# Last of eight experts written out, its rows placed by TensorE, and the meta rows dropped from layer two

## What is computed

```python
def first_block(x, meta_tokens, ...):
    h = jnp.concatenate([meta, x], axis=1)          # 16 + 256 rows
    for layer in range(2):                          # hybrid_layer
        h = hybrid_layer(h, ...)                    # q, k, v, z projections, causal attention of
                                                    # 4 "diff" and 8 "fox" heads, out projection
    return rms_norm(h, final_g)[:, N_META:]         # the 16 meta rows are dropped here

def second_block(x, ...):
    for l in range(2):
        x = x + mixers(rms_norm(x)) @ w_out[l]      # pooling, gated, convolution
        h = rms_norm(x)
        x = x + (swiglu(h) if l == 0 else moe_swiglu(h, ...))
    return rms_norm(x, final_g)

def moe_swiglu(h, router, wg, wu, wd):              # 8 experts, inner width 3584, top 2
    top_v, top_i = lax.top_k(t @ router, 2)
    top_w = softmax(top_v)
    for e in range(8):
        out = out + gates[:, e:e+1] * swiglu(t, wg[e], wu[e], wd[e])
```

## Time and profile before

| what | value |
|---|---|
| median of 3 runs | 1765.38 us (1765.19 to 1765.78) |
| the profiled execution, its own time | 1765.0 us |
| its span, first to last instruction | 1763.2 us |
| PE busy | 1686.0 us (96%), 10014 instructions |
| DVE, ACT, POOL busy | 1408.5, 1152.2, 253.0 us |
| DMA | 476.86 MB, mean 270 GB/s |
| granted TensorE clock, mean | 0.981 |

### The profile page before, as it was taken

The page is one execution under the profiler, slowest core; times in us unless marked ns, Lnnn a source line. Parts: engine busy times, 40 slices in busy tenths (PEclk is TensorE's granted clock), DMA queues, the critical chain, the costliest instruction groups (busy, mean ns, idle before and its releaser), DMA issues.

```text
span 1763.2 us, 27386 instructions
## 1 busy us (share of the span) xinstructions
PE 1686.0 (96%) x10014; PEld 1480.7 (84%) x10014; DVE 1408.5 (80%) x1607; ACT 1152.2 (65%) x1297; POOL 253.0 (14%) x261
## 2 busy tenths in 40 slices
PE   8999899989899999899999999999999999999993
PEld 7888898889799999788888888888888888888883
DVE  7666666759866667868898898988998988989885
ACT  5563555456654446677777777777777777777773
POOL 2212022128310003600010010000100100101000
PEclk9999999999899999999999999999999999999997
DMA  7322442245455464359999999999999999999993
GB/s 302 120 85 85 160 139 97 72 155 182 162 173 191 131 214 152 126 195 378 379 368 373 379 387 365 372 391 385 360 391 387 375 374 372 385 378 367 393 386 132
DMA packets 71329, 476.86 MB, mean 270 GB/s; under 512 B 8405, under 2 KB 9077, under 8 KB 19413
## 3 DMA queue, kind: packets, MB, share of 16 engines
q1 hardware_dynamic: 67781, 463.25, 70.0%
q0 software_dynamic: 3184, 11.55, 1.8%
q10 hardware_dynamic: 288, 1.05, 0.1%
HBM read 469.53 MB, written 6.29 MB: 270 GB/s over the span
## 4 chain that ended last, share of the span: by engine, by line
PE 75%; issue 9%; DVE 8%; ACT 3%; POOL 3%; DMA 1%; SPq 0%; DVEq 0%; POOLq 0%; ACTq 0%
PE bank L451 24%; PE bank L453 23%; PE bank L452 23%; DVE wlo L442 2%; ACT whi L437 2%; PE bank L1096 1%; POOL cacc L2234 1%; DVE msb L1747 1%; DVE bank L1777 1%; DVE sm L1667 0%; PE bank L730 0%; DMA ys<-y_slots 0%; POOL pr L2150 0%; PE bank L674 0%; PE bank L1068 0%
## 5 line engine op out<-in xcount | busy, mean ns | idle before, releaser
L442 DVE TENSOR_TENSOR wlo<-raw,whi 128x2048 fp32r<-128x2048 f32 (+2 forms) x453 | 1000.8, 2219 | 177.7 <-ACT whi L437 176.5
L437 ACT ACTIVATE whi<-raw 128x2048 fp32r<-128x2048 f32 (+2 forms) x453 | 838.0, 1850 | 219.0 <-PE bank L453 218.8
L451 PE MATMUL bank<-whi,hthi 128*128 128x512 f32 x896 | 354.1, 395 | 1.7 <-DVE htlo L2077 1.7
L453 PE MATMUL bank<-whi,htlo 128*128 128x512 f32 x896 | 350.1, 391 | 0.0
L452 PE MATMUL bank<-wlo,hthi 128*128 128x512 f32 x896 | 349.7, 390 | 0.0
L451 PE MATMUL bank<-uhi,whi 128*128 128x272 f32 (+2 forms) x1072 | 315.1, 294 | 4.0 <-DVE wlo L442 3.5
L453 PE MATMUL bank<-uhi,wlo 128*128 128x272 f32 (+2 forms) x1072 | 306.3, 286 | 0.0
L452 PE MATMUL bank<-ulo,whi 128*128 128x272 f32 (+2 forms) x1072 | 305.8, 285 | 0.0
L451 PEld LDWEIGHTS bank<-uhi,whi 128*128 128x128 f32 (+1 forms) x1072 | 201.9, 188 | 7.2 <-DVE wlo L442 4.8
L452 PEld LDWEIGHTS bank<-ulo,whi 128*128 128x128 f32 (+1 forms) x1072 | 202.3, 189 | 0.7
L453 PEld LDWEIGHTS bank<-uhi,wlo 128*128 128x128 f32 (+1 forms) x1072 | 202.1, 189 | 0.0
(11 more groups left out here) (354 smaller groups left out, 2128.6 us busy)
## 6 DMA issues: line engine op xcount, KB each, us to landing
raw<-in_wm SPq DMA_DIRECT2D x338, 1024.0 KB, 7.1
raw<-in_w SPq DMA_DIRECT2D x66, 1024.0 KB, 5.0
raw<-in_w SPq DMA_DIRECT2D x18, 768.0 KB, 4.3
raw<-in_w SPq DMA_DIRECT2D x16, 704.0 KB, 4.2
raw<-in_w SPq DMA_DIRECT2D x14, 512.0 KB, 3.6
ys<-y_slots SPq DMA_DIRECT2D x4, 512.0 KB, 5.3
raw<-in_w SPq DMA_DIRECT2D x2, 576.0 KB, 3.7
hT<-in_hT SPq DMA_DIRECT2D x2, 544.0 KB, 6.1
```

The costliest lines, as they stand in the source:

```text
L437: act.activation(whi[:, n % RING, 0:c], raw[:, n % RAW, 0:c], ACT.Copy).then_inc(hi_ready, 1)
L442: dve.tensor_tensor(wlo[:, n % RING, 0:c], raw[:, n % RAW, 0:c], whi[:, n % RING, 0:c].bitcast(F32), ALU.subtract).then_inc(lo_ready, 1)
L451: pe.matmul(out, s_hi, m_hi, start=start, stop=False, skip_group_check=shared)
L453: return pe.matmul(out, s_lo, m_hi, start=False, stop=stop, skip_group_check=shared)
```

## The change

1. *Layer two without meta rows.* In the second attention layer the q and z tiles, the output projection, and all that follows from them take columns 16 to 271 only (256 in place of 272), and the query tile of 16 rows is left out of scores, mask, exponent, scaling, turning and products. k, v and the logits keep 272.
2. *The last expert is written out.* All loops run seven turns; the eighth expert follows as straight code with `last=True`. It loads no ninth expert's units and gathers nothing. Ahead of it ACT and DVE read the count into a register. Its last two units are multiplied one output half at a time (`down_by_halves`), so both units must be split before the first product.
3. *Its rows reach the tokens through PE.* Its `yt` isn't scattered. PE turns its `pick` at chunk 4, DVE copies that to `pickT`, and after the last half PE makes four products (`place`) of `pickT` with `yt`, which DVE adds to `xt`.
4. *Other rows are added early.* SP loads `ys` behind its last weight unit, and DVE adds the slots to `xt` (`settle`) ahead of the last `yt`. Since the last expert's slots are not written any more, `y_slots` is cleared by POOL with four DMAs of 512 KB when the first mixer is done.
5. *The end.* Square sums are taken in halves of 512 columns, POOL scales the first half's sum, ACT loads its root table early.
6. The second loop keeps its place behind the branch and now prepares its own first expert.

```diff
+            take = leaving(l) if TILE_OF[i][0] in "qz" else slice(0, LEN)
             for k in range(KD):
-                    mm = three_pass(pe, bank[i % 2][:, 0:LEN], hi[:, k, cols], lo[:, k, cols],
-                                    uhi[:, k, :], ulo[:, k, :], k == 0, k == KD - 1)
+                    mm = three_pass(pe, bank[i % 2][:, take], hi[:, k, cols], lo[:, k, cols],
+                                    uhi[:, k, take], ulo[:, k, take], k == 0, k == KD - 1)
...
-            with sp.Fori(0, EXPERTS) as it:
+            with sp.Fori(0, LAST) as it:
                 expert(it)
-            sp.wait_ge(scattered, EXPERTS + 1)
+            expert(LAST, 0)
+            sp.wait_ge(scattered, EXPERTS)
+            load_rows()
             sp.wait_ge(count_ready, 1)
...
+                def down_by_halves(c):
+
+                    pe.wait_ge(atlo_ready, it * CHUNKS + (c + 1))
+                    views = [weights(EXPERT_UNITS.index(("down", c, part))) for part in range(2)]
+                    for half in range(2):
+                        cols = slice(half * 512, (half + 1) * 512)
+                        for part, (hi, lo) in enumerate(views):
+                            for i in range(2):
+                                f = 2 * part + i
+                                mm = three_pass(pe, bank[5 + half][:], athi[:, c % 2, f, :], atlo[:, c % 2, f, :], hi[:, i, cols], lo[:, i, cols],
+                                                False, f == 3)
+                        mm.then_inc(unit_done, 1)
...
+            def place():
+
+                pe.wait_ge(rows_ready, 5)
+                for tt in range(2):
+                    for half in range(2):
+                        pe.wait_ge(yt_ready, EXPERTS + half)
+                        pe.matmul(bank[2 * tt + half][:], pickT[:, tt * P:(tt + 1) * P], yt[:, half * 512:(half + 1) * 512],
+                                  start=True, stop=True).then_inc(placed, 1)
...
+            act.wait_ge(count_ready, 1)
+            fullest = act.value_load(cnti[0:1, 0:1], min_val=0, max_val=SEQ)
+            expert(LAST, True)
+            act.activation(warm[:, 7:8], eps[:], ACT.Sqrt)
             with act.If(fullest > P):
...
+            def settle(tt, times=1):
+
+                step = 4 * (times - 1) + 2 * tt
+                dve.wait_ge(ys_landed, 16 * 2 * TOP_K * times)
+                dve.tensor_tensor(ys[:, tt, 0, :], ys[:, tt, 0, :], ys[:, tt, 1, :], ALU.add).then_inc(result_step, 1)
+                dve.wait_ge(result_step, step + 1)
+                dve.tensor_tensor(xt[:, tt, :], xt[:, tt, :], ys[:, tt, 0, :], ALU.add).then_inc(result_step, 1)
...
             fullest = dve.value_load(cnti[0:1, 0:1], min_val=0, max_val=SEQ)
+            expert(LAST, True)
+            for tt in range(2):
+                dve.wait_ge(result_step, 2 * tt + 2)
+                for half in range(2):
+                    dve.wait_ge(placed, 2 * tt + half + 1)
+                    own = xt[:, tt, half * 512:(half + 1) * 512]
+                    dve.tensor_tensor(own, own, bank[2 * tt + half][:], ALU.add).then_inc(sum_ready, 1)
+            dve.wait_ge(sum_ready, 4)
             with dve.If(fullest > P):
...
+                if L == 0:
+                    pool.wait_ge(unit_done, UNIT_FF)
+                    pool.memset(zero[:], 0.0).then_inc(const2_ready, 1)
+                    pool.wait_ge(const2_ready, CONST2 + 1)
+                    clear_slots(zero)
```

## The result

The changed kernel takes 1740.78 us (median of 4 runs, 1740.44 to 1742.14), the kernel before on the same chip 1765.58 (1765.19 to 1766.0): a ratio of 0.9861, 95% interval 0.9844 to 0.9878. A second set on another chip gave 1739.66 and 0.9866 (0.985 to 0.9883). The profiled execution has a span of 1738.8 us against 1763.2, 24.4 us less.

What follows compares the result with a forecast made beforehand. PE was taken as the bound in the experts and mostly in layer two, then 27.3 us of end chain without PE. Span 1763.2 - 7.0 + 1.0 - 13.6 = 1743.6, plus 2.2 is 1745.8 us; range 1739.5 to 1754.5.

Steps and rivals of the forecast that it cites:

- better than forecast: Rival, chance 0.07: register load costs nothing, branch 0.1 us, attention brings 10 us; 1740.4 us.
- Layer two, -7.0: Second attention layer without meta rows: columns 4.9 us and query tile 3, less 0.9 given back; minus 7.0 us.
- The 0.9 us given back to DVE: Layer two's output projection: PE's tiles get shorter, DVE's splits do not, so DVE may be late; 0.9 us lost.
- Ahead of the experts, 0: Between layer two and the first expert: the forecast's sum has no term for any change there.
- Register load, +1.0: Start of last expert: ACT's and DVE's register read delays splits and PE; 1.1 less 0.1 slack, plus 1.0 us.
- Code of the last expert, 0: Last expert written out: its new code must be fetched, but PE does not wait for it; nothing taken.
- Dropped `gather`, -0.7: Last expert: two times four transposes of the ninth expert's `gather` leave PE, 0.35 us each.
- The stand-still of 2.2 us: Last two units: PE waits 2.2 us for the second split; `settle` and this stall hide each other almost exactly.
- The end, from the last split to the last scaling: After the last split: `place`, adds, square, root, DVE's branch at 1.5 us, then scaling ending at 1746.55.
- The rival with register loads and branches at their upper ends: Upper bounds of 2.5 us for the last expert's register load and for the end's branch; no chance given.
- the starving expert: Rival, chance 0.03: last expert's written-out code waits for instruction packets, 3 us each; slower, 1772.8 us.
- attention giving nothing: Rival, chance 0.13: other engines set layer two's pace, so savings on PE become longer waits; 1752.8 us.

Runs made afterwards that it cites:

- e1: Changed kernel with the second attention layer computing all 272 columns and the 16-row query tile again: 1750.27 us.
- e2: Changed kernel with 272 columns kept in the second attention layer, only the 16-row query tile dropped: 1745.55 us.
- e0: The changed kernel itself run again on another chip, nothing altered: 1739.66 us, 0.9866 of the kernel before.
- e8: Changed kernel with four more register loads on both ACT and DVE where the last expert begins: 1743.67 us.
- e7: Changed kernel with the last two experts written out, so the loops run six turns: 1742.03 us.
- e5: Changed kernel with both `settle` calls moved behind the last `yt`: 1745.81 us, ratio 0.9908 to the kernel before.
- e3: Changed kernel with ACT's early load of the root table moved behind its branch: 1742.19 us.
- e9: Changed kernel with `y_slots` cleared twice, eight DMAs of 512 KB on POOL's queue in place of four: 1742.92 us.
- e10: Changed kernel with ACT's root table loaded behind its branch, the same edit run once more on another chip: 1740.64 us.
- e4: Changed kernel with the last two units multiplied in the loop's plain order in place of by halves: 1743.96 us.
- e6: Changed kernel with half of `settle` on POOL, last two units in plain order, root table loaded behind ACT's branch: 1741.82 us.

## Why the prediction was right or wrong, point by point

The forecast was 1745.8 us with a range of 1739.5 to 1754.5; 1740.8 lies in the range, near its lower end, almost exactly where the rival "better than forecast" stood (1740.4, chance 0.07), and outside the 1742.5 to 1749.5 that had 0.60. It got there only in part for that rival's reasons: the register load cost nothing, but the branch was not 0.1 and 1.1 us is luck of the clock.

- **Layer two, -7.0: mis-sized, -8.8 (against e1) to -9.6 (against the kernel before).** The columns came near (2.7 to 4.4 for 4.9). The tile was taken at 3 of its 4.8 us on the ground that small forms overlap with neighbours; e2 puts it at 4.4 to 6.1. The 0.9 us given back to DVE wasn't given back: the waits are the same.
- **Ahead of the experts, 0: another 1.4.** Between the end of layer two and the first expert the shift grows from 9.7 to 11.1, 0.2 by the second mixer and 1.1 at the first expert. The 1.1 is the stretch at half clock behind PE's wait for `htlo`, which the kernel before has in its trace and the changed kernel by chance has not (e0). The prediction names that wait but had not read the clock behind it.
- **Register load, +1.0: wrong, 0.06** (the splits' shift goes from 11.08 to 11.02 there). The step that failed was to price it by SP's 2.47 us as "load, comparison and branch together", and to say that no row shows a load alone. The trace of the kernel before has such rows on the queues, SP's ahead of the 2.47 us and DVE's at the end of the loop:

```profile
L574 SPq TENSOR_LOAD <-cnti x1: 475/475/475, 1742.8 to 1742.8; - x1
L2126 DVEq TENSOR_LOAD <-cnti x1: 555/555/555, 1736.1 to 1736.1; - x1
```

  The 2.47 us, from 1743.73, are what follows SP's branch. DVE's load runs at 1736.1 while the engine is on its splits (1732.89 to 1737.47), so the cover too could be read there. A first load takes some 0.8 us with its register work and is hidden while its engine works (e8). The Trainium skill ("Runtime: NRT & Kernel Launch", Instruction fetch mechanics) has about 0.2 us for a register; the rows show 0.30 to 0.56 for the load and 0.18 to 0.22 behind it.
- **Code of the last expert, 0: right** (e7). Dropped `gather`, -0.7: right, 11.0 becomes 11.8.
- **The stand-still of 2.2 us: right, 2.14**, and that `settle` and it hide each other: right (e5). Missed: the clock can halve behind a stand-still, here within 1.5 us of its end. In the traces with PE waiting there it did so in e2, e7 and e8 (tails of 17.07, 17.26, 17.08) and not in the changed kernel, e0, e1, e3, e5, e9 and e10. Where the wait stands ahead of `place` it did so in e4 and not in e6 (2.32 us). It costs 1.6 us when it comes. That the stand-still is the cause is argued, not shown by an experiment of its own. What speaks for it is that from the first expert to these waits, where PE goes on all but without a stop, none of the thirteen traces has a halved stretch. Why it comes in some executions only stays open.
- **The end, from the last split to the last scaling:** forecast 15.92 us (1745.27 less 1729.35), measured 15.45. The four products: 3.85 as forecast (4 x 0.95 = 3.8, the first one included). The branch: 1.5 forecast, 0.72 measured (e10); of the 0.8 us between them 0.6 were taken up again by a thing not forecast, a table load of 1.28 us between square and root (e3, e10). That the warming activation stands ahead of the branch and not behind it was in the diff, and I counted it as done. I had read the 2.47 us of SP as a price of any engine's branch; each has its own.
- **Store, 3.05: 4.2 in this execution**, since landing took 4.4 us in place of 2.6. e0 had 2.6.

In all, in span: 11.1 us were gained by the first expert (forecast 7.0), less 0.1 for the register load (forecast 1.0), and 13.4 at the end with `gather` and the store (forecast 13.6): 24.4 (forecast 19.6). So of the 4.8 us that the forecast fell short, 2.6 lie in layer two, 1.4 between it and the first expert, most of it luck, and 0.9 in the register load, less 0.2 at the end.

The rival with register loads and branches at their upper ends is refuted by e7 (leaving the loop), e8 (loads) and e10 (branch), the starving expert by e7, attention giving nothing by e1. None of the variations beats the changed kernel as a total (e10 has 0.9876 of the kernel before, the changed kernel 0.9861 and 0.9866); e3's edit is 0.6 us better in the tail, below what totals can tell.

## What to carry to other kernels

Where an engine sets the pace and hardly waits, price dropped work at its full distance on that engine, small forms too, and take the discount for overlap only where the trace shows a neighbour that fills the gap. A register load ahead of a branch is paid for by its queue, not by its engine, as long as instructions of the engine are still running; look at the queue's rows (load, register work, branch) before pricing it. Load an activation table behind the last branch and behind the last use of another table; and look at the granted clock behind every stand-still of PE near 2 us, in the kernel before too: here the products behind it ran at half clock in some executions, which cost 1.1 to 1.6 us, and two traces compared can differ by that alone.

## What was not expected of the hardware

- After 2.1 us of standing still near the end PE's granted clock fell to 0.5, 1.2 GHz, for one stretch of 3.4 us in four traces (e2, e7, e8, e4) and stayed at 1.0 in the eight others, e6 with 2.3 us among them: products 0.43 us apart for 0.23, `place` 5.37 us for 3.85. At the first expert it did so in nine of eleven traces, after 1.7 to 2.2 us.
- DVE instructions that began beside POOL's float32 adds of 128 x 1024 (4.2 and 4.3 us) ended their usual time after POOL's add had ended: 3.19 us for 2.29 and 3.41 for 1.22 (e6).
- A branch over a body that is skipped cost DVE 0.72 us to its next instruction (e10), SP 2.5 us.
- Squares run on the root's table where that was loaded behind the branch (e3, e10). With the loading ahead of the branch, the first square brings a table of its own and the root loads its own again, 1.28 us each.
- The same two stores of 512 KB landed after 2.6 to 2.8 us in twelve traces and after 3.8 and 4.4 in one.
